# Experts of a routed layer walked in an order found on the chip: small, large, small, large

## The reference

```python
D_MODEL, SEQ, N_EXPERTS, TOP_K, D_EXPERT = 1024, 512, 32, 4, 1024      # batch 1, one layer, float32
mod = silu(c) @ w_ada + b_ada            # shift, scale and gate of the mixer and of the expert part
h = modulate(rms_norm(x, norm_mix_pre), shift_m, scale_m);  u = h @ w_in
ya = rg_lru(causal_conv(xa)) * gelu(ga);  yb = causal_pool_mixer(xb)
x = x + gate_m * rms_norm(concatenate([ya, yb]) @ w_out, norm_mix_post)
h = modulate(rms_norm(x, norm_ffn_pre), shift_f, scale_f)
logits = h @ router_w + router_b;  top_val, top_idx = top_k(logits, 4);  gates = softmax(top_val)
# for each token and each of its 4 experts e:
#   u = h @ w1[e] + b1[e]                                   (1024 -> 2048)
#   glu = min(u[::2], 7);  lin = clip(u[1::2], -7, 7)
#   y = (glu * sigmoid(1.702 * glu) * (lin + 1)) @ w2[e] + b2[e]          (1024 -> 1024)
f = sum over the 4 of gate * y
out = x + gate_f * rms_norm(f, norm_ffn_post)
```

## Time and profile before

| | us |
|---|---|
| median of three runs | 1470.37 |
| profiled execution: its own time | 1479.31 |
| its span, first to last instruction | 1477.6 |
| first bias matmul of the expert part starts | 270.9 |
| last down matmuls end | 1418.5 |
| PE busy | 1231.0 (83%) |
| DMA: 462.84 MB | mean 313 GB/s |

### The profile page before, as it was taken

One profiled execution on the slowest core, in us unless ns is written; L12 is line 12 of the kernel. 1 busy time (PEld: TensorE's weight loads), 2 busy tenths in 40 slices (PEclk: granted clock), 3 DMA queues, 4 the chain that ended last, 5 costly groups with the idle time before them and its releaser, 6 DMA issues.

```text
span 1477.6 us, 28341 instructions
## 1 busy us (share of the span) xinstructions
PE 1231.0 (83%) x8843; PEld 416.9 (28%) x8844; DVE 412.6 (28%) x864; ACT 217.1 (15%) x481; POOL 276.5 (19%) x421
## 2 busy tenths in 40 slices
PE   4999995468998999877757999986799889989961
PEld 1434455112332333221212333321223223322320
DVE  3215336212232232211112222321132222222317
ACT  2108532001110111100001101110011011101101
POOL 3032001201222122211101211321021112211212
PEclk9899995688999999988868999998799999999975
DMA  9882514597659588899999970599998997899354
GB/s 323 308 298 115 235 43 185 222 420 297 243 209 420 226 357 341 361 419 421 419 421 420 419 306 25 236 387 420 400 404 363 421 421 325 328 421 421 139 212 183
DMA packets 77461, 462.84 MB, mean 313 GB/s; under 512 B 11924, under 2 KB 12052, under 8 KB 29312
## 3 DMA queue, kind: packets, MB, share of 16 engines
q1 hardware_dynamic: 49280, 314.72, 52.5%
q10 hardware_dynamic: 17568, 126.14, 20.7%
q0 software_dynamic: 10592, 21.72, 4.3%
HBM read 453.08 MB, written 16.91 MB: 318 GB/s over the span
## 4 chain that ended last, share of the span: by engine, by line
PE 68%; DMA 15%; DVE 6%; SPq 5%; issue 3%; ACT 3%; POOLq 1%; ACTq 0%; POOL 0%; DVEq 0%
PE bank L1418 33%; PE bank L1446 18%; DMA W<-in_expert_w 12%; SPq L372 5%; PE bank L1293 4%; PE bank L1335 4%; PE bank L1427 2%; PE bank L1497 2%; DMA W<-in_w_ada 2%; PE bank L1253 1%; PE bank L1406 1%; DVE W L1217 1%; DVE OV L1139 1%; DMA OV<-h_rows,src_cur 1%; DMA W<-y_rows 1%
## 5 line engine op out<-in xcount | busy, mean ns | idle before, releaser
L1418 PE MATMUL bank<-W,OV 128*32 128x512 f32 x5056 | 577.0, 609 | 50.9 <-DMA W<-in_expert_w 50.9
L1446 PE MATMUL bank<-W,OV 128*32 128x512 f32 x2528 | 320.4, 652 | 46.2 <-ACT OV L798 22.3
L1418 PEld LDWEIGHTS bank<-W,OV 128*32 128x32 f32 x5056 | 157.3, 111 | 444.8 <-issue 362.7
L1139 DVE TENSOR_TENSOR OV<-bank,OV 128x512 f32<-128x512 f32 x79 | 54.6, 692 | 487.1 <-PE bank L1418 481.5
L1446 PEld LDWEIGHTS bank<-W,OV 128*32 128x32 f32 x2528 | 83.4, 117 | 228.1 <-issue 189.7
L1152 DVE COPY OV<-bank 64x512 f32<-64x512 f32 x79 | 54.8, 693 | 298.8 <-PE bank L1446 298.8
L580 POOL DMA_INDIRECT OV<-h_rows,src_cur x104 | 106.3, 1022 | 61.8 <-POOL src_cur L575 42.7
L575 POOL COPY src_cur<-OV 128x2 int32 (+1 forms) x52 | 11.3, 218 | 522.6 <-PE bank L1406 492.9
L793 ACT ACTIVATE OV<-OV 128x256 f32<-128x256 f32 x79 | 35.3, 447 | 466.7 <-DVE OV L1141 456.7
L1427 PE MATMUL bank<-ident,store 128*128 128x128 f32 x216 | 48.8, 314 | 48.8 <-DVE store L1147 47.9
L1293 PE MATMUL bank<-W 128*128 128x512 f32 x192 | 85.1, 596 | 0.0
(11 more groups left out here) (230 smaller groups left out, 674.2 us busy)
## 6 DMA issues: line engine op xcount, KB each, us to landing
W<-in_expert_w SPq DMA_DIRECT2D x252, 1024.0 KB, 14.8
W<-in_expert_w ACTq DMA_DIRECT2D x120, 1024.0 KB
W<-in_w_ada SPq DMA_DIRECT2D x24, 1024.0 KB, 7.1
W<-y_rows SPq DMA_DIRECT2D x4, 2048.0 KB, 14.7
W<-in_w_in SPq DMA_DIRECT2D x3, 2048.0 KB, 11.6
W<-in_w_out SPq DMA_DIRECT2D x1, 4096.0 KB, 16.1
store<-in_x SPq DMA_DIRECT2D x4, 512.0 KB, 5.2
h_rows<-W POOLq DMA_DIRECT2D x4, 512.0 KB, 3.3
```

The costliest lines, as they stand in the source:

```text
L1139: TTo(u_sb[:, hf, :], bank[hf][:, :], b1_cur, ALU.add).then_inc(u_ok[hf], 1)
L1418: last = mm(bank[hf][H * j:H * j + H, :], xT[:, hf, k % QM, H * (k // QM):H * (k // QM) + H], W1[:, slot, k, UW * j:UW * j + UW], start=(k ...
L1446: last = mm(bank[4 + hf][H * j:H * j + H, :], gT[:, hf, r, H * c:H * c + H], W2[:, c, r, HW * piece:HW * piece + HW], start=(c == 0), stop ...
```

## The change

The halves of each expert are counted as before. A key of halves x 32 less the expert's number, with the first expert's set to the lowest, is compared with all keys; the count of greater ones is the expert's rank. An expert of rank r gets place 2r + 2 or 2(n - r) - 1, whichever is less, where n is the number of experts with rows other than the first; the first gets place 0. So places 1, 3, 5 are taken by the smallest, 2, 4, 6 by the largest. Experts without rows get a place under zero and stand in no list. PE turns places and steps into each expert's first step and into the list by place (`counts`: steps, halves, full steps, the expert's number). `counts` is written ahead of the slots. All engines walk the places instead of the numbers; SP, ACT and DVE read the expert's number from the list. The first expert stays the one with number 0, whose weights are loaded ahead.

```diff
+        by_expert = take(8)                       # in the upper half of W1's slot 1, behind bc
+        steps_by = take(1)
+        key_row, compare, before_row = take(E), take(E), take(E)
+        place = take(NPOS)                        # NPOS = E + 1
+        iota_id = take(1)
...
 @block.sync
-            load = sp.value_load(counts[0:1, 3, 1:2], min_val=0, max_val=16)
+            load = steps_of(1)                    # value_load of counts[0:1, 0, i]
+            second = expert_at(1)                 # value_load of counts[0:1, 3, i]
             with sp.If(load > 0):
                 for k in range(HALF):
-                    load_w1(sp, 1, 1, k)
+                    load_w1(sp, second, 1, k)
             sp.wait_ge(idx_ok, 1)
...                                               # the other half likewise
-                    load = sp.value_load(counts[0:1, 3, bass.ds(e, 1)], min_val=0, max_val=16)
+                    load = steps_of(e)
+                    expert = expert_at(e)
...
-                            load_w1(sp, e, slot, k)
+                            load_w1(sp, expert, slot, k)
 @block.gpsimd
+            nc.gpsimd.iota(iota_id, [[0, 1]], base=0, channel_multiplier=1, **IMP).then_inc(route_const, 1)
 @block.scalar
-                load = act.value_load(counts[0:1, 3, bass.ds(e + 1, 1)], min_val=0, max_val=16)
+                load = act.value_load(counts[0:1, 0, bass.ds(e + 1, 1)], min_val=0, max_val=T // (2 * H))
+                following = act.value_load(counts[0:1, 3, bass.ds(e + 1, 1)], min_val=0, max_val=E - 1)
...
-                        load_w2(act, e, part, w2_v[1:E])
+                        load_w2(act, following, part)
 @block.vector
-            link(nc.vector.tensor_copy(exp_f[:, 0, :], exp_i[:, 2, :]))
-            link(nc.vector.tensor_tensor_scan(exp_f[:, 1, :], ones[:, 0:E], exp_f[:, 0, :], 0.0, ALU.mult, ALU.add))
-            link(TTo(exp_f[:, 2, :], exp_f[:, 1, :], exp_f[:, 0, :], ALU.subtract))
-            link(TS(exp_f[:, 3, :], exp_f[:, 2, :], float(2 * H), None, ALU.mult))
+            link(nc.vector.tensor_copy(halves_f, exp_i[0:E, 1, :]))
+            link(STT(key, halves_f, float(E), iota_e[0:E, :], ALU.mult, ALU.subtract))
+            link(nc.vector.memset(key[:, 0:1], -2.0 * E))
+            link(TTo(cmp, key, diag, ALU.mult))
+            link(nc.vector.reduce_sum(by(4), cmp, axis=AX.X))
+            link(TS(cmp, key, by(4), None, ALU.is_gt))
+            link(nc.vector.reduce_sum(by(5), cmp, axis=AX.X))
+            link(TS(cmp, key, 0.0, None, ALU.is_gt))
+            link(nc.vector.reduce_sum(by(6), cmp, axis=AX.X))
+            link(TTo(by(7), by(6), by(5), ALU.subtract))
+            link(TS(by(7), by(7), 2.0, -1.0, ALU.mult, ALU.add))
+            link(TS(by(5), by(5), 2.0, 2.0, ALU.mult, ALU.add))
+            link(TTo(by(5), by(5), by(7), ALU.min))
+            link(STT(by(3), ident[0:E, 0:1], 0.0, by(5), ALU.is_equal, ALU.mult))
+            link(TTo(cmp, exp_i[0:E, 2, :], diag, ALU.mult))
+            nc.vector.reduce_sum(steps_by[0:E, :], cmp, axis=AX.X).then_inc(place_ok, 1)
+            dve.wait_ge(place_ok, 1)
+            link(TTo(cmp, halves_f, diag, ALU.mult))
+            link(nc.vector.reduce_sum(by(0), cmp, axis=AX.X))
+            link(STT(by(2), by(0), 1.0, ident[0:E, 0:1], ALU.min, ALU.max))
+            link(nc.vector.tensor_copy(by(1), iota_id[0:E, :]))
+            TS(place[0:E, :], iota_q[0:E, 0:NPOS], by(3), by(2), ALU.is_equal, ALU.mult).then_inc(place_ok, 1)
+            dve.wait_ge(pos_ok, 1)
+            TS(before_row[0:E, :], bank[6][0:E, 0:E], by(3), None, ALU.is_gt).then_inc(rows_ok, 1)
+            dve.wait_ge(start_ok, 1)
+            link(TS(exp_f[:, 3, :], bank[6][:, 64:64 + E], float(2 * H), None, ALU.mult))
...                                               # slots of the tokens, as before (L1083 to L1092)
+            link(nc.vector.memset(counts[:, :, :].rearrange("p a e -> p (a e)"), 0))
+            dve.wait_ge(list_ok, 1)
+            link(nc.vector.tensor_copy(counts[0:1, 1, :], bank[5][0:1, 64:64 + NPOS]))
+            nc.vector.tensor_copy(counts[0:1, 3, :], bank[5][0:1, 128:128 + NPOS]).then_inc(counts_ok, 1)
+            link(TS(counts[0:1, 0, :], counts[0:1, 1, :], 1, None, ALU.add))
+            TS(counts[0:1, 0, :], counts[0:1, 0, :], 1, None, ALU.arith_shift_right).then_inc(counts_ok, 1)
+            TS(counts[0:1, 2, :], counts[0:1, 1, :], 1, None, ALU.arith_shift_right).then_inc(counts_ok, 1)
+            dve.sem_inc(counts_ok, 1)
             for n in range(TK):                   # the 16 pairs of slot operations
...                                               # behind them, the 7 operations L1098 to L1104 go
+            def select(i, slot):
+                e = dve.value_load(counts[0:1, 3, i], min_val=0, max_val=E - 1)
+                TS(sel_e[:, slot, :], same_j, hot_row[:, bass.ds(e, 1)], None, ALU.mult).then_inc(sel_e_ok, 1)
 @block.tensor
+            pe.wait_ge(place_ok, 1)
+            mm(bank[6][0:E, 0:E], by_expert[0:E, 3:4].to_broadcast([E, E]), ident[0:E, 0:E], ...).then_inc(pos_ok, 1)
+            pe.wait_ge(place_ok, 2)
+            pe.wait_ge(rows_ok, 1)
+            mm(bank[6][:, 64:64 + E], steps_by[0:E, :].to_broadcast([E, P]), before_row[0:E, :], ...).then_inc(start_ok, 1)
+            for v in range(2):
+                last = mm(bank[5][0:1, 64 + 64 * v:...], by_expert[0:E, v:v + 1], place[0:E, :], ...)
+            last.then_inc(list_ok, 1)
```

More of the change, by code:

```diff
@@ L39, in hybrid_layer @@
     VECS = 72
+    NPOS = E + 1
     h_rows = nc.dram_tensor("h_rows", (T * J, QW), fp32).ap()
@@ L181, in hybrid_layer @@
         idx_n = take(NQ).bitcast(i32)
+        take = carver(B_hi[:, KT * T + 3 * D:])
+        by_expert = take(8)
[3 more added lines that the diff above has]
+        iota_id = take(1)
         take = carver(OV)
@@ L196, in hybrid_layer @@
         idx = take(2, NQ // 2, 2).bitcast(i32)
-        counts = OV[0:1, 6656 - 4 * E:6656].rearrange("p (a e) -> p a e", a=4).bitcast(i32)
+        counts = OV[0:1, 6656 - 4 * NPOS:6656].rearrange("p (a e) -> p a e", a=4).bitcast(i32)
         y_all = carver(flat(W1[:, 1, :, :]))(TT, TOPK, D)
@@ L291, in hybrid_layer @@
         b1_in = sem("b1_in")
+        place_ok = sem("place_ok")
+        pos_ok = sem("pos_ok")
+        rows_ok = sem("rows_ok")
+        start_ok = sem("start_ok")
+        list_ok = sem("list_ok")
         bias_const = sem("bias_const")
@@ L424, in _, with steps_of, expert_at @@
                 sp.sem_inc(w1_in[1][k], 16)
-            load = sp.value_load(counts[0:1, 3, 1:2], min_val=0, max_val=16)
+            def steps_of(i):
+                return sp.value_load(counts[0:1, 0, bass.ds(i, 1)], min_val=0, max_val=T // (2 * H))
+            def expert_at(i):
+                return sp.value_load(counts[0:1, 3, bass.ds(i, 1)], min_val=0, max_val=E - 1)
+            load = steps_of(1)
+            second = expert_at(1)
             with sp.If(load > 0):
                 for k in range(HALF):
-                    load_w1(sp, 1, 1, k)
+                    load_w1(sp, second, 1, k)
             sp.wait_ge(idx_ok, 1)
@@ L438, in _ @@
             sp.reg_mov(landed[1], 16)
-            sp.reg_add(landed[1], landed[1], load)
+            with sp.If(load > 0):
+                sp.reg_add(landed[1], landed[1], 16)
+            sp.nop()
             def add_steps(e):
@@ L1035, in route_tile @@
                     dve.wait_ge(router_in, 32)
-                    dve.wait_ge(route_const, 5)
+                    dve.wait_ge(route_const, 6)
                 link(TTo(logits[:, i, :], logits[:, i, :], router_bias, ALU.add))
@@ L1077, in _, with by @@
             link(TS(exp_i[:, 2, :], exp_i[:, 0, :], 1, None, ALU.arith_shift_right))
-            link(nc.vector.tensor_copy(exp_f[:, 0, :], exp_i[:, 2, :]))
-            link(nc.vector.tensor_tensor_scan(exp_f[:, 1, :], ones[:, 0:E], exp_f[:, 0, :], 0.0, ALU.mult, ALU.add))
-            link(TTo(exp_f[:, 2, :], exp_f[:, 1, :], exp_f[:, 0, :], ALU.subtract))
-            link(TS(exp_f[:, 3, :], exp_f[:, 2, :], float(2 * H), None, ALU.mult))
+            def by(n):
+                return by_expert[0:E, n:n + 1]
@@ new lines, in _ @@
+            halves_f, diag = exp_f[0:E, 0, :], ident[0:E, 0:E]
+            key, cmp = key_row[0:E, :], compare[0:E, :]
+            link(nc.vector.tensor_copy(halves_f, exp_i[0:E, 1, :]))
[4 more added lines that the diff above has]
+            link(TS(cmp, key, by(4), None, ALU.is_gt))
@@ L1096, in _ @@
                     .then_inc(slots_ok, 1)
[L1098 to L1105, removed]
             dve.wait_ge(top_exp, 1)
@@ L1156, in finish @@
                 TTo(y_sb[hf], bank[4 + hf][0:YP, :], y_part[hf], ALU.add).then_inc(y_ok[hf], 1)
-            def select(e, slot):
-                TS(sel_e[:, slot, :], same_j, hot_row[:, e], None, ALU.mult).then_inc(sel_e_ok, 1)
+            def select(i, slot):
```

(17 more changed lines are left out.)

## The result

The changed kernel takes 1421.28 us in the median of four runs (1417.88 to 1422.26) against 1470.43 for the kernel before beside it: a ratio of 0.9652, 95% interval 0.9623 to 0.9681. Two later jobs gave 0.9660 (0.9636 to 0.9684) and 0.9674 (0.9657 to 0.9690). The forecast was 1394, its own range 1383 to 1407: the direction was right, but instead of a gain of 76 us there was one of 49.

A forecast was written before the change was run, and what follows sets the result against it. Mostly PE work bounds it, with 12% waiting for expert weights; loads cost 110 of 1147.6 us. Routing, gathers and expert windows put the last down's end at 1341.8 instead of 1418.7, rounded -76: 1394, range 1383 to 1407.

The forecast's parts named there:

- Routing: Sort and counts block before the index table: +5.0 us, bounds +3 and +8.
- Gathers: First row gathers, now beside the second expert's early weight loads: +3 us, bounds 0 and +7.
- First two experts: Start of the walk: first expert 20.1 us without the empty turn, second about free at 17.6.
- Smalls behind nine, seven, five and three fours: Six one-half experts behind larges of those many halves: 17.6 us each, W2 hidden, 105.6 in all.
- rival of one buffer biting behind fours and fives: W2's single buffer makes four more smalls take 24.5 us instead of 17.6: 28 more, 1422; chance 0.15.
- Smalls behind threes: Three one-half experts behind three-half ones, W1 and W2 sharing queues: 24.54 us each, 73.5 in all.
- Larges: Experts of three to nine halves from the nine on: free prices, no load waits, 640.3 us in all.
- Twos: Seven experts of two halves: 29.4 us each as today, not due to loads, 205.8 in all.
- The base: Profiled execution of 1479.31 us, 9 over the median 1470.37; a difference was said to carry over.
- slower streaming: Rival: loads at 404 to 407 GB/s add nothing; only under some 390 do they, 1496 at 336; chance 0.02.
- no reordering: Rival: ranks give about today's order, only the early fetch counts: 1472; chance 0.02.
- a slower kernel: Rival: smalls behind larges find both weights late, 36.43 us each, 167 more: 1561; chance 0.03.

The follow-up runs named there:

- W2 first: Changed kernel, but SP issues W1 of place e only once the third W2 piece of place e - 2 has landed: 1402.26, 1401.25 and 1401.75 us.
- floor run: Changed kernel, but from the third place on each W1 piece loads only its first 256 of 2048 columns: 1377.16 us, ratio 0.9301.
- before4: The kernel before, unchanged, profiled again in a job without the 1.2 us lags: 1469.76 us.
- falling order: Changed kernel with places in falling order of halves after the first expert (9, 7, 5, fours, threes, twos, ones): 1499.04 us, ratio 1.0190.

## Why the prediction was wrong, point by point

All terms are set against the profile after. The last down matmul was forecast for 1341.8 and ended at 1361.8, 20.0 later. The step that failed is the overlap of a small expert's W2 with its own up part: the prediction held it to be hidden, and it was not. The three terms that rest on it miss by 7.7, 13.4 and 8.6 us.

- **Routing**, +5.0 to the index table: the sort cost 4.5, the counts' move nothing as said, and POOL copied the first indices 4.6 later. **Gathers**, +3: 4.2 (9.47 against 5.25), inside the bounds. First bias 278.9 against 279.7. Right.
- **First two experts**: the first 20.1 against 19.65, the missing empty turn paid. The second 17.6 against 25.30, +7.7. **Here the step failed**: "Its four pieces land by about 302, 307, 312, 314.6". PE got the last of them at 322.77 (first row below, the changed kernel). I had counted three pieces of the next W1 (the nine's) as out, but not the W1 after it, which the second expert's own up matmuls release while its W2 is still coming. With that one held back (second row, W2 first) PE has the last piece at 318.44 and the window is 21.97. In the floor run, where the nine's W1 is thin as well, it is 17.50. So 3.3 of the 7.7 us are the W1 after next, and the rest goes only when the nine's own W1 is thinned too; how far that is a wrong count of its pieces no run separates.

```profile
322.77 1.94 PE L1509 MATMUL bank<-W,OV 128*32 128x512 f32 x8 [3.79 <-DMA W<-in_expert_w]
...
318.44 1.06 PE L1511 MATMUL bank<-W,OV 128*32 128x512 f32 x8 [1.41 <-DMA W<-in_expert_w]
```

- **Smalls behind nine, seven, five and three fours**, 105.6 against 119.0, +13.4: the same omission. The failed words are "W2 alone (10 us) lies under the small one's 12 us". Behind the nine and the seven it didn't matter (17.72, with ACT's earlier issue), behind the five it cost 1 us, behind the fours 4 us each. W2 first shows it: with that W1 held back these six windows are 16.19 to 18.74 and the whole 20.3 us less. The rival of one buffer biting behind fours and fives came true at half its price (13 us instead of 28). That its 1422 is the measured time is luck: the second expert and the larges made up the rest.
- **Smalls behind threes**, 73.5 against 73.6: right, since the price was a measured window of the same place, sharing included.
- **Larges**, 640.3 against 648.9, +8.6: put at nothing without a reason. PE waits for W2 at the end of a late small one, and the large one behind it starts at the lower granted clock. The first 4 us of the first three are at 0.51, almost wholly at 1.2 GHz; the three takes 38.40 and the nine 106.26. Length times missing clock, summed over the seven larges below 1.00, gives these 8.6 us. In the floor run, with hardly any late weights, a three is 36.45 and the nine 104.56, at 1.00.

```profile
832.90:836.90 4.00, 4.00 (x14) 0.51 1.01 422
```

- **Twos**, 205.8 against 195.4, -10.4. "That is not the load" was right, but 29.4 held the 1.2 us lag of the profiled chip. Before4 has 26.5 to 28.3, and 30.56 for the two behind a small one.
- **The base.** The sum was made against an execution of 1479.3 with the lags, while the measured pair had none. The base's walk then ends at 1409.5 (before4) and not at 1418.7, 9.3 earlier. But the seven twos of the forecast carried the same lags: by before4 they are 196.5 and not 205.8. Both ends move by 9.3, and "a difference carries over" held. On like terms the forecast gain stays 76.9 and the measured one is 47.6 (1409.5 less 1361.8). The 29.3 missing are the 7.7, 13.4 and 8.6 above, less small rests. The 27 between 76 and 49 are these 29.3 less 2 in the tail and rounding.
- The rivals of slower streaming (418 to 421 GB/s in the windows shown after at a DMA share of 1.01 or 1.02), of no reordering and of a slower kernel fell. The Trainium skill, "DMA: Bandwidth & Descriptors", section "Where 436 GB/s comes from", has the HBM side bind at about 358 GB/s; these windows do not agree with it. How an order does become slower was seen in falling order: not by both weights late behind each large, but by loads with nothing to hide them at the end.

## What to carry to other kernels

When single and double buffers feed from shared queues, list for each load everything that is released while it is out, the present item's own releases first; a small item frees its slot just when its own second weight is needed. Alternating long and short work pays where the short one's loads lie under the long one's work, and a fixed priority (the weight needed next goes first) gave back another 1.4% for two lines. Price a place by a measured window of the same neighbourhood where there is one, and give a long item behind a stalled short one its start at the lower clock. Compare two kernels on one chip.

## What the runs showed of the hardware

Chips of one kind differ in one small thing: on two of five the last activation of a pair of halves started 1.2 us behind the modelled end of its last matmul, nine times in the kernel before, which took 10 us (0.7%) longer there; on three never. The changed kernel was timed on chips without it alone. It stood in the forecast's base and in its twos alike, so it does not explain the miss; its cause was not tried.
